# A fused token-mixing layer on one core: filling products, three moved steps and stores issued from another engine

## The reference, cut to what matters

```
h    = rms_norm(x, pre_norm)                      # (4096, 1024)
proj = h @ w_in                                   # 3*1024 mixer + 1536 gate + 512 memory query columns
b, c, u = split(proj[:, :3072])
z    = c * u
mix  = b * (w0*z[t-2] + w1*z[t-1] + w2*z[t])      # short convolution over tokens
k, v = split(rms_norm(mem, mem_norm) @ w_mem_kv)  # 256 memory rows, 4 heads of 128
mem_o = softmax(q @ k.T / sqrt(128)) @ v          # q: the last 512 columns of proj
y    = (concat[mix, mem_o] * silu(gate)) @ w_out  # 1536 -> 1024
out  = x + rms_norm(y, post_norm)
```

## Time and profile before

| what | value |
| --- | --- |
| median of three executions | 2220.6 us |
| the profiled execution, its own time | 2222.47 us |
| its span | 2220.6 us |
| PE busy | 2191.1 us (99%) |
| DVE busy | 1218.6 us (55%) |
| ACT busy | 739.1 us (33%) |
| POOL busy | 100.8 us (5%) |
| DMA moved | 468.95 MB, mean 211 GB/s |
| the three matmul lines of `product` on the chain that ended last | 87% |

### The profile page before, as it was taken

The page is one execution under the profiler, slowest core; times in us unless marked ns, Lnnn a source line. Parts: engine busy times, 40 slices in busy tenths (PEclk is TensorE's granted clock), DMA queues, the critical chain, the costliest instruction groups (busy, mean ns, idle before and its releaser), DMA issues.

```text
span 2220.6 us, 27170 instructions
## 1 busy us (share of the span) xinstructions
PE 2191.1 (99%) x10106; PEld 1821.0 (82%) x10106; DVE 1218.6 (55%) x1933; ACT 739.1 (33%) x1332; POOL 100.8 (5%) x155
## 2 busy tenths in 40 slices
PE   9999999999999999999999999999999999999998
PEld 7888888788888887888888888888888788888886
DVE  7677867644244352444335328675754755555554
ACT  5343433411221331212113333535452533333332
POOL 0000000000000000000000000100000000000000
PEclk9999999999999999999999999999999999999999
DMA  3786677667666778856667665656667633334331
GB/s 140 276 308 234 256 276 258 239 232 249 205 209 217 263 263 314 305 190 208 209 209 258 226 215 195 221 199 220 198 206 296 220 125 110 119 133 133 129 123 63
DMA packets 144737, 468.95 MB, mean 211 GB/s; under 512 B 15808, under 2 KB 15840, under 8 KB 141280
## 3 DMA queue, kind: packets, MB, share of 16 engines
q1 hardware_dynamic: 123808, 391.70, 50.1%
q0 software_dynamic: 20800, 75.53, 10.4%
HBM read 330.85 MB, written 136.31 MB: 210 GB/s over the span
## 4 chain that ended last, share of the span: by engine, by line
PE 89%; DVE 5%; DMA 3%; issue 2%; ACT 1%; SPq 0%; POOL 0%; DVEq 0%; ACTq 0%; POOLq 0%
PE banks L1541 29%; PE banks L1543 29%; PE banks L1542 29%; DVE hop_lo L1146 2%; DMA slots<-w_split 1%; PE banks L1658 1%; DMA sums_kept<-raws 1%; PE banks L1714 1%; DVE x_in L1132 1%; DMA q_kept<-zb 0%; ACT probs L917 0%; PE banks L1562 0%; ACT hop_hi L849 0%; DVE rmax L1295 0%; PE banks L1547 0%
## 5 line engine op out<-in xcount | busy, mean ns | idle before, releaser
L1541 PE MATMUL banks<-hop_hi,slots 128*128 128x512 f32 x2632 | 1030.8, 392 | 10.3 <-DMA slots<-w_split 5.1
L1542 PE MATMUL banks<-hop_lo,slots 128*128 128x512 f32 x2632 | 1024.7, 389 | 0.0
L1543 PE MATMUL banks<-hop_hi,slots 128*128 128x512 f32 x2632 | 1024.6, 389 | 0.0
L1541 PEld LDWEIGHTS banks<-hop_hi,slots 128*128 128x128 f32 x2632 | 494.3, 188 | 117.2 <-issue 10.1
L1543 PEld LDWEIGHTS banks<-hop_hi,slots 128*128 128x128 f32 x2632 | 494.1, 188 | 103.3
L1542 PEld LDWEIGHTS banks<-hop_lo,slots 128*128 128x128 f32 x2632 | 494.4, 188 | 101.2 <-issue 1.4
L1174 DVE TENSOR_TENSOR slots<-raws,slots 128x512 fp32r<-128x512 f32 x156 | 106.8, 690 | 141.2 <-ACT slots L804 140.7
L860 ACT ACTIVATE s<-banks 128x512 f32<-128x512 f32 x94 | 56.3, 599 | 302.3 <-PE banks L1543 301.5
L1226 DVE TENSOR_TENSOR u<-banks,u 128x512 f32<-128x512 f32 x54 | 37.3, 690 | 213.9 <-PE banks L1543 213.9
L804 ACT ACTIVATE slots<-raws 128x512 fp32r<-128x512 f32 x156 | 96.8, 626 | 153.6 <-PE banks L1543 128.6
L804 ACT ACTIVATE slots<-st_w 128x512 fp32r<-128x512 f32 x144 | 90.2, 627 | 153.6 <-PE banks L1543 114.4
(11 more groups left out here) (169 smaller groups left out, 2085.4 us busy)
## 6 DMA issues: line engine op xcount, KB each, us to landing
slots<-w_split SPq DMA_DIRECT2D x406, 512.0 KB, 3.5
w_split<-slots SPq DMA_DIRECT2D x140, 512.0 KB, 3.0
raws<-in_w_in SPq DMA_DIRECT2D x86, 256.0 KB, 4.0
x_in<-in_x_t SPq DMA_DIRECT2D x16, 1024.0 KB, 7.2
g_kept<-mix POOLq DMA_DIRECT2D x32, 512.0 KB, 6.3
raws<-g_kept SPq DMA_DIRECT2D x64, 256.0 KB, 3.9
x_zb<-in_x POOLq DMA_DIRECT2D x22, 512.0 KB, 4.4
out_x<-x_zb POOLq DMA_DIRECT2D x21, 512.0 KB, 4.1
```

Source lines behind the costliest of these rows:

```text
L1541: nc.tensor.matmul(dst, a, c, start=first, stop=False, skip_group_check=True)
L1542: nc.tensor.matmul(dst, a, d, start=False, stop=False, skip_group_check=True)
L1543: return nc.tensor.matmul(dst, b, c, start=False, stop=last, skip_group_check=True)
```

## The change

- `WARM` goes from (50, 16) to (24, 12) filling matmuls.
- `SUMS_LOAD_AT` goes from steps 1, 11, 21, 31 of macro 2 to steps 92, 102, 112, 122; the subtractions (three steps later) and the stores (eight steps later) go with it.
- Sum 2 of a macro's end stands on DVE in step R7, behind the rest of hop R6, instead of in step R3.
- `keep` moves from POOL to ACT. There it stands in step R5 of the next pair, behind ACT's copy of R5 (and for pairs 0 and 1 in the start, for the last pair in the second step of the output stage). The stores of the gated memory heads (`keep_gated`) stay on POOL.
- In the last pair DVE's R2 add and the norm's `finish` of the second last block of 128 tokens stand ahead of the addition L1509 instead of behind it.

```diff
-WARM = (50, 16)
+WARM = (24, 12)
...
-SUMS_LOAD_AT = [1 + 10 * k for k in range(HK)]
+SUMS_LOAD_AT = [92 + 10 * k for k in range(HK)]
 SUMS_AT = [a + 3 for a in SUMS_LOAD_AT]
 SUMS_KEEP_AT = [a + 8 for a in SUMS_LOAD_AT]
...
         def _(pool):
...
-            def keep(p):
-                m, i, kind = p // PAIRS, row_of(p), kind_of(p)
-                if kind == "q":
-                    pool.wait_ge(c12_done, seven_to(p))
-                    pool.wait_ge(c22_done, seven_to(p))
-                    pool.wait_ge(c11_done, seven_to(p))
-                    pool.wait_ge(copied, count("qcy", p) + 1)
-                    pool.dma_start(kept_as(q_kept, m, i - FIRST_Q), zb[:, :, HALO:]).then_inc(q_kept_dma, 16)
...
-            for p in range((MACROS - 1) * PAIRS):
-                keep(p)
-            for step in range(PAIRS * PRODUCTS):
-                p, r = divmod(step, PRODUCTS)
-                if r == R5 and p:
-                    keep((MACROS - 1) * PAIRS + p - 1)
-                for n in range(HEADS):
-                    if step == WEIGH_AT[n] + 1:
-                        keep_gated(n)
-            keep(ALL_PAIRS - 1)
+            for n in range(HEADS):
+                keep_gated(n)
...
         def _(act):
...
+            def keep(p):
+                m, i, kind = p // PAIRS, row_of(p), kind_of(p)
+                if kind == "q":
+                    act.wait_ge(c12_done, seven_to(p))
+                    act.wait_ge(c22_done, seven_to(p))
+                    act.wait_ge(c11_done, seven_to(p))
+                    act.wait_ge(copied, count("qcy", p) + 1)
+                    act.dma_start(kept_as(q_kept, m, i - FIRST_Q), zb[:, :, HALO:]).then_inc(q_kept_dma, 16)
+                if kind == "m":
+                    act.wait_ge(silu_done, silu_count(p, R4))
+                    act.dma_start(kept_as(m_kept, m, i), zb[:, :, HALO:] if p == 1 else mix[:]).then_inc(m_kept_dma, 16)
+                if kind == "g":
+                    group = (i - FIRST_C) // 4
+                    act.wait_ge(gated, 4 * (count("g", p) + 1))
+                    for f in range(2):
+                        act.dma_start(g_kept[...], ...).then_inc(g_kept_dma, 16)
...
             operand_hi(0, R7)
+            keep(0)
...
             operand_hi(0, R4)
+            keep(1)
...
                     evacuate(p, r)
+                    if r == R5 and p > DIRECT:
+                        keep(p - 1)
                     ahead(m, step)
...
                     evacuate(p, r)
+                if n == 1:
+                    keep(ALL_PAIRS - 1)
...
-                        if r in (R6, R3):
-                            token_sum(m + 1, {R6: 1, R3: 2}[r])
+                        if r in (R6, R7):
+                            token_sum(m + 1, {R6: 1, R7: 2}[r])
...
-                if n and OUT_STEPS[n - 1][1] == M1:
+                if n and OUT_STEPS[n - 1][1] == M1 and p < LAST_PAIR:
                     finish(2 * (OUT_STEPS[n - 1][0] - ALL_PAIRS))
+                if (p, r) == (LAST_PAIR, M1):
+                    add(p, R2)
+                    finish(2 * (p - ALL_PAIRS))
...
                 for output in (R3, R7, R2):
-                    if UNIT_OF[p, r] == done_with(p, output):
+                    if UNIT_OF[p, r] == done_with(p, output) and (p, output) != (LAST_PAIR, R2):
                         add(p, output)
```

More of the change, by code:

```diff
@@ L712, in _ @@
                                pattern=[[-1, P]], channel_multiplier=1).then_inc(consts_set, 1)
-            def kept_as(kept, m, f):
-                return kept[m, 2 * f:2 * f + 2].rearrange("f t p n -> p (f t) n")
-            def keep(p):
-                m, i, kind = p // PAIRS, row_of(p), kind_of(p)
-                if kind == "q":
-                    pool.wait_ge(c12_done, seven_to(p))
-                    pool.wait_ge(c22_done, seven_to(p))
-                    pool.wait_ge(c11_done, seven_to(p))
-                    pool.wait_ge(copied, count("qcy", p) + 1)
-                    pool.dma_start(kept_as(q_kept, m, i - FIRST_Q), zb[:, :, HALO:]).then_inc(q_kept_dma, 16)
-                if kind == "m":
-                    pool.wait_ge(silu_done, silu_count(p, R4))
-                    pool.dma_start(kept_as(m_kept, m, i), zb[:, :, HALO:] if p == 1 else mix[:]).then_inc(m_kept_dma, 16)
-                if kind == "g":
-                    group = (i - FIRST_C) // 4
-                    pool.wait_ge(gated, 4 * (count("g", p) + 1))
-                    for f in range(2):
-                        pool.dma_start(g_kept[2 * SUB * m:2 * SUB * (m + 1), group // 2, :, group % 2 * 2 + f, :].rearrange("s p n -> p s n"),
-                                       flat(mix[:, 2 * f:2 * f + 2, :]).rearrange("p (s n) -> p s n", n=P)).then_inc(g_kept_dma, 16)
             def keep_gated(n):
```

4 lines of the change are left out of this document (added).

## The result

| kernel | median us | range | runs |
| --- | --- | --- | --- |
| before | 2221.0 | 2219.6 to 2224.8 | 19 |
| after | 2228.0 | 2223.5 to 2232.6 | 19 |

The ratio is 1.0029, 95% interval 1.0023 to 1.0035: by the ratio 6.4 us slower (the medians lie 7.0 apart), where 2216.3 us, 4.3 less than before, was forecast and 2212.0 to 2220.0 was the range. The profiled execution of after took 2232.55 us for a span of 2230.7, the slowest of the 19, so its waits are rather large; its span is 10.1 us longer than before's.

A forecast was written before the change was run, and what follows sets the result against it. PE is busy 99% of the span, so time changes only where PE waits. Terms -4.4 - 3.9 + 2.7 + 0.3 + 0.2 + 0.8 + 0.5 - 0.5 = -4.3 took 2220.6 to 2216.3 us; range 2212.0 to 2220.0.

The forecast's parts named there:

- The stores from ACT: Issue at macro ends +0.3, attention +0.2, later landing at start of macro 3 +0.8, start of output stage +0.5 us.
- Rival C: Macro ends and macro 3: query stores landing beyond 8.0 us delay DVE's add of R3; 12.9 us more, 2229.2; chance 0.05.
- The 40 other stores: Stores besides the queries': +0.2 us for convolution stores in the attention, +0.5 for the last store at the output stage's start.
- The sums: Macro 2: output weights' sums at later steps remove PE's waits of 1.57 and 2.32 us for weights; -3.9 us.
- rival D: Macro 2: stores of the sums again take 7.6 us, loads come late as before; 2220.2 us, chance 0.10.
- Token sum 2: Macro ends: moving this sum makes sum 3 and ACT's copy of R6 0.9 us later each time; +2.7 us.
- rival A: Macro ends: moving sum 2 is free, the 2.04 us wait goes for good; 2210.3 us, chance 0.10.
- The start: Before the first product: fewer filling products let PE take the sums sooner, first product at 20.7 us; -4.4 us.
- Rival B: Start, 11.5 to 15.5 us: PE's clock falls back with little work, losing say 2 us; 2218.3, chance 0.13.
- The last norm: After the last product: earlier finish lets L1526 wait for ACT instead of DVE; -0.5 us.

The follow-up runs named there:

- experiment 7: Changed kernel with all stores on POOL, those of the memory gate and gated convolution held back until ACT's copy of R5 in the next pair: ratio 0.9996.
- experiment 1: Changed kernel with the stores of rows back on POOL, all else as after: 2214.7 us, ratio 0.9970.
- experiment 8: Four versions of the changed kernel, stores on POOL, sum 2 at its old place, varying fills and sums' steps: 2213.5, 2214.1, 2213.1, 2212.7 us.
- experiment 2: Kernel before with only the last norm's finish moved ahead of the addition of M1: 2217.0 us, ratio 0.9983.

## Why the prediction was wrong

- **The stores from ACT: the step that failed.** The terms for it were 0.3 + 0.2 + 0.8 + 0.5 = 1.8 us, and they are 13.1: 8.7 for the queries and 6.4 for the others, each measured apart. Without them the forecast was 2216.3 - 1.8 = 2214.5, and that kernel takes 2214.7. That it fits so well is in part luck: the start gained 1.2 us less, the sums gave 1.0 back, and the end gained 3.3 more. In the stores' terms the issue was right (0.1 us beside the copy). The landing of the queries was mis-sized: at the macros' ends it stood at nothing, as landing within 8.0 us, and it took 9.45 and 9.70. Rival C had the right mechanism for the queries and nearly the right point: free up to 8.0 us of landing, where the trace gives 9.45 - 1.67 = 7.8 (it leaves 2.6 us sooner than I wrote, and the deadline is as much sooner). That its time fits too (2229.2 against 2228.0) is luck: it wanted 12.9 us of the queries alone, 2.9 of them at the end of macro 0, where the store landed in 4.7 and cost nothing, and it had nothing for the other 40 stores. I held it for unlikely since the DMA engines are less busy there than at the 7.63 of the earlier trace rows. But that store came from SP's own queue in one order with the loads; from another queue in 528 packets it took 9.4 and 9.7. The chance of 0.05 was too small. At the start of macro 3 I took 6.8 us for the landing; it was 10.06, and behind the wait of 4.17 us the granted clock fell to 0.50 too.
- **The 40 other stores** had 0.2 us for ACT's time and 0.5 for the last one, and no term for what their new moment meets: the store of the sums at 1084 us, the load of the memory's weights at 1275. They cost 6.4 us.
- **The sums.** With the stores on POOL the term of -3.9 holds for the most part (-4.5 and +1.0 to +2.6). In after +4.1 came back: rival D, but for another reason, since with the store of g late the store of the sums lands late (experiment 7, where +3.2 comes back by that alone).
- **Token sum 2.** +0.9 at each macro's end in experiment 1, for 0.9 each. Right, as far as traces tell; rival A is dead.
- **The start.** -3.2 for -4.4. Rival B came true (0.50 granted from 13.4 to 20.0 us), its cost was 0.6 to 1.2 us (experiment 8) for the 2 us that it named, and it can be avoided.
- **The last norm.** 0.5 us of SP's store were right, but 3.3 more came from POOL's last store, which I had not followed.

Open are the late units near 1690 us. They cost 1.2 to 2.9 us more than in before in every kernel with fewer fills or with all stores from ACT, and nothing more in the three that have neither: the sooner finish alone, the later sums alone and the queries held back on POOL. Open is also what happens in the 8.8 us behind POOL's last store. That the last output block could be stored from SP instead was not tried.

## What to carry to other kernels

A store moved to another queue is not priced by the time of its issue: ask when it now leaves, what else is under way then, into how many packets that queue cuts it (here 528 from ACT and 272 from POOL for the same megabyte), and which instruction waits for its landing with how much in hand; a landing measured in another queue is no bound (7.63 us in SP's, 9.45 and 9.70 in ACT's). Ask the same of the small stores: here 40 of them with a term of 0.7 us cost 6.4. Where the deciding point of a mechanism (8.0 us) lies 0.4 us from a landing that the trace shows (7.63), its chance is not 0.05. And follow each engine to its last instruction: the end may hang on the one that seems idle, as here on POOL's last store, 8.8 us ahead of it (experiment 2).

## What the runs showed of the hardware

- The span ended 8.8 to 8.9 us behind POOL's last DMA issue in all twenty traces, while SP's last row of stores stood 3.7 to 7.0 us from the end.
- One megabyte from the same tile into the same array was 528 packets from ACT and 272 from POOL. The DMA engines were busy for the same share of the span with all 33.6 MB of these stores (4.6% from ACT, and q0 went from 10.4% to 5.8%), so by this share the smaller packets cost no engine time.
- The wait of 2.04 to 2.10 us at the end of macro 0 is there in twelve traces. In three of them the granted clock fell behind it (0.68 between 415 and 420 us in experiment 2), which cost 1.6 us, of which 0.6 came back at the next wait for `u`; in nine it stayed at 1.00, before among them. The same wait thus costs 2.0 or 3.0 us. And the 3.07 us at 1103 in after brought no fall (1.00 from 1103.4 to 1112 us).
